# Where the old state of a chunked recurrence is added: in the PSUM accumulators or on VectorE

## The reference, cut to what matters

```python
def wkv_scan(r, w, k, v, a, bb, s0, reverse):
    def step(s, inp):
        r_t, w_t, k_t, v_t, a_t, b_t = inp
        sa = jnp.einsum("bhvk,bhk->bhv", s, a_t)
        s = s * w_t[:, :, None, :] + sa[..., None] * b_t[:, :, None, :] + v_t[..., None] * k_t[:, :, None, :]
        return s, jnp.einsum("bhvk,bhk->bhv", s, r_t)
    ...
    s_fin, o = lax.scan(step, s0, xs, reverse=reverse)
    return s_fin, jnp.moveaxis(o, 0, 1)
```

## Time and profile before

| what | us |
|---|---|
| median of 3 runs (lowest, highest) | 3789.93 (3787.76, 3793.22) |
| the profiled execution, own time | 3785.12 |
| its span | 3783.3 |
| TensorE busy in the span | 3357.8 (89%) |
| VectorE busy in the span | 2569.7 (68%) |
| ScalarE busy in the span | 1265.4 (33%) |

### The profile page before, as it was taken

The page is one execution under the profiler, slowest core; times in us unless marked ns, Lnnn a source line. Parts: engine busy times, 40 slices in busy tenths (PEclk is TensorE's granted clock), DMA queues, the critical chain, the costliest instruction groups (busy, mean ns, idle before and its releaser), DMA issues. The chain is left out here.

```text
span 3783.3 us, 67165 instructions
## 1 busy us (share of the span) xinstructions
PE 3357.8 (89%) x28642; PEld 2684.9 (71%) x28642; DVE 2569.7 (68%) x3589; ACT 1265.4 (33%) x2021; POOL 269.8 (7%) x235
## 2 busy tenths in 40 slices
PE   2999898999757877869999999989977999999997
PEld 1888686887426777737888888767735777888885
DVE  7566447572456676645977777767786588777777
ACT  2211222223434333323422222235465443222223
POOL 0000000000000000000111111020000001111110
PEclk9999999999869899979999999999968999999998
DMA  4233311132382233132111111111000121111111
GB/s 186 98 111 114 133 62 45 67 108 82 134 282 55 58 82 82 49 141 86 54 51 57 61 51 51 39 46 34 18 12 1 62 72 51 52 51 51 51 51 56
DMA packets 151062, 278.38 MB, mean 74 GB/s; under 512 B 9836, under 2 KB 82684, under 8 KB 150508
## 3 DMA queue, kind: packets, MB, share of 16 engines
q1 hardware_dynamic: 135468, 244.50, 19.5%
q10 hardware_dynamic: 15296, 29.57, 2.2%
HBM read 228.11 MB, written 45.65 MB: 72 GB/s over the span
## 5 line engine op out<-in xcount | busy, mean ns | idle before, releaser
L2518 PE MATMUL PS<-ffn_x_low_again,ring_b_wh 128*128 128x512 f32 x1120 | 436.0, 389 | 0.0
L2517 PE MATMUL PS<-ffn_x_high,ring_b_wh 128*128 128x512 f32 x1120 | 436.0, 389 | 0.0
L2767 DVE SCALAR_TENSOR_TENSOR xT<-xT,PS 128x1024 f32<-128x1024 f32 (+1 forms) x320 | 368.2, 1162 | 5.3 <-PE PS L2527 0.2
L248 DVE TENSOR_TENSOR ring_a_wl<-ring_a_raw,ring_a_wh 128x1024 fp32r<-128x1024 f32 x72 | 88.2, 1225 | 340.2 <-ACT ring_a_wh L245 339.9
L2750 DVE TENSOR_TENSOR xT<-xT,PS 128x512 f32<-128x512 f32 x280 | 188.1, 683 | 120.6 <-PE PS L2519 119.1
L245 ACT ACTIVATE ring_a_wh<-ring_a_raw 128x1024 fp32r<-128x1024 f32 x72 | 76.1, 1058 | 571.5 <-PE PS L282 547.2
L2525 PE MATMUL PS<-ffn_hid_high,ffn_down_high 128*128 128x512 f32 x640 | 253.2, 396 | 3.7 <-DVE xT L2767 3.2
L245 ACT ACTIVATE ring_b_wh<-ring_b_raw 128x512 fp32r<-128x512 f32 (+1 forms) x156 | 120.4, 773 | 388.7 <-PE PS L2519 252.9
L2526 PE MATMUL PS<-ffn_hid_low,ffn_down_high 128*128 128x512 f32 x640 | 250.3, 391 | 0.0
L2527 PE MATMUL PS<-ffn_hid_high,ffn_down_raw_again 128*128 128x512 f32 x640 | 250.2, 391 | 0.0
L2517 PEld LDWEIGHTS PS<-ffn_x_high,ring_b_wh 128*128 128x128 f32 x1120 | 210.3, 188 | 43.7
(11 more groups left out here) (507 smaller groups left out, 7767.3 us busy)
## 6 DMA issues: line engine op xcount, KB each, us to landing
ffn_down_raw<-in_ffn_down SPq DMA_DIRECT2D x40, 512.0 KB, 3.5
scan_tin<-scan_in SPq DMA_DIRECT2D x36, 512.0 KB, 5.3
norm_e_t<-in_ada SPq DMA_DIRECT2D x32, 512.0 KB, 4.0
ring_a_raw<-in_in_o SPq DMA_DIRECT2D x32, 512.0 KB, 4.4
ring_b_raw<-in_ffn_up SPq DMA_DIRECT2D x58, 256.0 KB, 4.5
ring_b_wl_again<-in_ffn_up SPq DMA_DIRECT2D x56, 256.0 KB, 4.3
scan_in<-um SPq DMA_DIRECT2D x20, 641.0 KB, 9.4
ring_a_raw<-in_in_e SPq DMA_DIRECT2D x24, 512.0 KB, 3.5
```

The costliest lines, as they stand in the source:

```text
L2517: nc.tensor.matmul(out, wh[:, k, :], xh[:, o, k], start=k == 0, stop=False)
L2518: nc.tensor.matmul(out, wh[:, k, :], xl[:, o, k], start=False, stop=False)
L2767: nc.vector.scalar_tensor_tensor(x, x, ALPHA if q == N_PLAIN else 1.0, out, ALU.mult, ALU.add)\
```

## The change

The old state enters PSUM by products: ahead of the growth's first `across`, the identity (128 x 128) times the state of each direction (128 x 256) goes into banks 2 and 3 with `start=True`, and both halves of the growth accumulate on it. VectorE's addition is gone; its scaling now reads the banks instead of `ST`.

```diff
@@ -1569,11 +1569,9 @@
                                     next(ahead, None)
                                 dve.wait_ge(S["u_done"], g * (4 * NC) + (4 * c + 4))
                                 st = ST[:, :, :, :]
-                                link(nc.vector.tensor_tensor(st.rearrange("p d j v -> p d (j v)"),
-                                                             st.rearrange("p d j v -> p d (j v)"), two_banks(2, 256),
-                                                             ALU.add))
                                 factor = fold[:, p, 1] if c == 0 else fold[:, 1 - p, 0]
-                                nc.vector.tensor_tensor(st, st, factor.unsqueeze(3).to_broadcast([P, 2, JB, HALF]),
+                                grown = two_banks(2, 256).rearrange("p d (j v) -> p d j v", j=JB)
+                                nc.vector.tensor_tensor(st, grown, factor.unsqueeze(3).to_broadcast([P, 2, JB, HALF]),
                                                         ALU.mult).then_inc(S["st_ready"], 1)
                             for _ in ahead:
                                 pass
@@ -1852,9 +1850,12 @@
                                 if not last_turn:
                                     turn_over(g + 1, 1 - p, 4 * c, 4 * c + 2)
                                 if not end:
+                                    for d in range(2):
+                                        nc.tensor.matmul(bank(2 + d, 256), ident[:, :], ST[:, d].rearrange("p j v -> p (j v)"),
+                                                         start=True, stop=False, skip_group_check=True)
                                     across(2, lambda j, h, d: tok[halves[d], p, T_K, c, j, halves[h]],
                                            lambda j, h, d: tok[halves[d], p, T_V, c, j, halves[h]], None, False,
-                                           stop=False, begin=True)
+                                           start=False, stop=False)
                                 pe.wait_ge(S["sa_ready"], g * NC + (c + 1))
                                 if not end:
                                     across(2, lambda j, h, d: tok[halves[d], p, T_B, c, j, halves[h]],
```

## The result

The changed kernel's median is 3803.71 us (6 runs) against 3792.35 for the kernel before (6 runs): ratio 1.0032, 95% interval 1.0021 to 1.0042, that is 8 to 16 us slower. In a second measurement it was 3795.57 (11 runs) against 3785.06 (24 runs), ratio 1.0027 (1.0017 to 1.0037), 6 to 14 us. The forecast was 3800 us (+10.3) with a range from 3792 to 3806.

What follows compares the result with a forecast made beforehand. In main turns' state parts TensorE was taken to work without pause, VectorE's update hidden. Updates summed to +11.3 us, stops took off 1.0: 3789.9 + 10.3 = 3800 us, range 3792 to 3806.

Steps and rivals of the forecast that it cites:

- The price of a pair: Two wide products ahead of the growth: four records 0.21 us apart, as at line 212, so 0.85 us.
- Hidden whole in main turns: VectorE's 1.42 us update in main turns delays nothing; slack before the state's products grows from 0.8 to about 1.5 us.
- Context turns: Updates of turns 0 and 1: first chunks +0.15 us each, second chunks, up to the masks, -0.2 each.
- Last turn: First chunk's update: the wait for SA partly covers the products, growth only some 0.4 us later; -0.3 us.
- The tie at the masks: Second chunks of turns 2 to 8: VectorE and TensorE arrive together at the next masks; some 0.2 us gained in all.
- TensorE's stops: Waits for the next instruction in the scan: four of the 14 main-turn places have one that pays, 1.05 us together.
- the rival's mechanism: Instruction pieces arrive on their own schedule, so later stops in the scan pay 6.7 us: +4.6, 3794.5 us; chance 0.18.
- the 11.3 - 1.0 of the sum: All updates: +11.7 main turns, +0.3 and -0.4 context turns, -0.3 last turn, less 1.0 from stops; net +10.3 us.
- that clock rival: In the scan, added TensorE work keeps the clock up and gives the loss back, 3789.6 us; chance 0.08.
- a growth of 1.7 us a turn: Sign of being right: from turn 2 to turn 9 the distance of like places grows so much, less stops.
- a scan longer by under 5 us: Sign of being wrong: if the scan grows by less than this, the sum was wrong in its main term.
- the main term: The 14 updates of main turns 2 to 8: TensorE pays 0.85 us each, less 0.2 in all, +11.7 us.

Runs made afterwards that it cites:

- no_add: Kernel before without the addition and without the wide products, so the old state is left out of the new one: 3781.36 us, ratio 0.9991.
- add_kept: Kernel before with the wide products put in front of the growth, which overwrites them, and VectorE's addition kept: 3796.89 us, ratio 1.0032.
- twice: Changed kernel with each pair of wide products issued twice: 3807.95 us, ratio to the kernel before 1.0059.
- the two context kernels: `context_ahead` and `context_only`, the kernel before with the change in the two context turns alone: 3789.10 and 3794.56 us.
- outputs_later: Kernel before with the second chunk's output products behind the next turn's first 16 products and remaining decays behind VectorE's third mask: 3784.53 us, ratio 0.9983.
- later_and_context: `outputs_later` plus the wide products in the two context turns, ahead of the wait for Z: 3782.08 us, ratio to the kernel before 0.9974.
- ahead_of_z: Changed kernel with the wide products one place earlier, ahead of the wait for Z: 3796.23 us, ratio to the kernel before 1.0020.
- context_ahead: Kernel before with the change in the two context turns alone, wide products ahead of the wait for Z: 3789.10 us, ratio 1.0001.
- context_only: Kernel before with the change in the two context turns alone, products at the change's place: 3794.56 us, ratio 1.0018.

## Why the prediction was right, point by point

*The price of a pair*: 0.85 forecast from line 212, 0.86 to 0.87 measured, and 0.87 for a second one. From the first wide record to line 1812 pass 0.95 us (1376.03 to 1376.98), not the 0.85 that the prediction named as a sign: the step from a wide product to the quarter products takes 0.31. But the wide products start 0.11 behind the last transpose, where the growth started 0.20 behind it, and 0.95 + 0.11 - 0.20 = 0.86.

*Hidden whole in main turns*: shown three ways. `no_add` leaves A at 3.93 where no stop stands, `add_kept` costs what the changed kernel costs, and the state is ready 1.05 us early. Forecast was a slack of 1.5; it is smaller because in this turn the stops went: from the copy of SA, the update starts 0.91 us later than before (3.09 against 2.18), but TensorE's next state product only 0.43 (4.83 against 4.40).

*Context turns*: A in turn 1 went from 3.74 to 3.89 (+0.15, as forecast; in the changed kernel's third profile it is 4.85, at a mean granted clock of 0.81 in that stretch). From SA to the masks it went from 3.00 + 2.32 to 3.86 + 1.25, -0.21 (forecast -0.2).

*Last turn*: A from 3.15 to 3.10, -0.05 (forecast -0.3): the update starts 2.26 us behind the copy of SA instead of 1.59, 0.67 later where 0.4 was forecast. Here, too, the pair stands between quarter products. Before, with the rest in the earlier trace rows:

```profile
1631.07 0.28 PE L1814 MATMUL PS<-tok 64*64 64x64 f32 x2
...
1631.43 0.69 DVE L1563 COPY SA<-PS 128x512 f32<-128x512 f32 x1 [1.59 <-PE PS L1739]
...
1631.97 0.38 PE L1814 MATMUL PS<-tok 64*64 64x64 f32 x9 [0.28 <-issue]
```

And in the changed kernel:

```profile
1638.26 1.13 PE L1854 MATMUL PS<-ST,ident 128*128 128x256 f32 x4
1638.37 0.69 DVE L1563 COPY SA<-PS 128x512 f32<-128x512 f32 x1 [2.02 <-PE PS L1737]
...
1639.32 0.69 PE L1812 MATMUL PS<-tok 64*64 64x64 f32 x32
...
1639.84 0.65 PE L1812 MATMUL PS<-SA,tok 64*64 64x64 f32 x32
```

The growth's first half starts 0.95 behind the start of the copy of SA instead of 0.36 ahead of it, 1.31 later and not 0.85. The half that reads SA starts 1.47 behind it instead of 0.75: the wait for SA, with a stop inside it, covered 0.6 us.

*The tie at the masks*: forecast -0.2 in seven turns. The distance from line 1731 to the masks adds up to 10.3, 10.9 and 10.2 us in turns 3 to 9 before, and 9.4 and 10.0 after: -0.8. Only a small part of that is the tie. In the first profile VectorE is late for the masks of turns 4 (1.39) and 6 (1.26), 0.15 us together, as forecast (the prediction counts by the turn before, 3 and 5). The rest are stops of TensorE inside the products that the masks wait for, in turn 7 before (2.64, 2.92 and 2.10 in the three profiles) and in turn 3 after (1.93 and 2.48), of which the prediction's list of turns says nothing. Turn 7 before, and turn 3 after:

```profile
1491.68 1.54 PE L1731 MATMUL PS<-AR,Bc 64*64 64x128 f32 x48 [1.20 <-issue]
...
1492.46 1.33 DVE L1509 COPY_PREDICATED LMB<-masks,PS 128x1024 f32<-128x1024 int32 x1 [1.74 <-PE PS L1731]
```

```profile
1283.83 1.31 PE L1729 MATMUL PS<-AR,Bc 64*64 64x128 f32 x36 [0.37 <-issue]
...
1284.30 1.34 DVE L1509 COPY_PREDICATED LMB<-masks,PS 128x1024 f32<-128x1024 int32 x1 [1.72 <-PE PS L1729]
```

In the other turns after, the context turns among them, the distance is 1.25.

*TensorE's stops*, the term that was mis-sized. Over turns 2 to 8, A adds up to 28.8, 29.4 and 28.9 us before and 34.1 and 34.4 after, +5.2; B to 29.8, 29.4 and 30.3 against 33.6 and 33.6, +3.8. Fourteen pairs at 0.86 would be 12.0, so 3.0 us were paid from stops inside the state parts, not 1.0. The prediction took the idle time that the profile notes for the price of a stop, and a stop lengthens its part by more. In turn 4 a stop of 0.16 is noted, but A is 4.40, 0.47 over the 3.93 of a part without one. The four places that the prediction counted with 1.05 us are 0.36, 0.47, 0.75 and 0.43 over 3.93, 2.0 together. Five more are 0.13 to 0.41 over it, 1.4 together, with no stop noted there or one under the 0.15 from which the views note idle time. All of them lie behind the product's place. In the changed kernel they are gone, and one new stop stands ahead of the place, in turn 8 (A 5.19 and 5.47). With 0.86 us more in each part the next piece seems to arrive in time; `twice`, with 1.73 more, has no stop in these parts either. That is the rival's mechanism at less than half of its size (6.7). Over the whole scan the noted stops fell by little, from 30.5 us in the mean to 29.2, so whether the 3.0 us were saved or part of them came back in the first parts of the turns is open.

Together the state parts and masks give +8.2 in main turns and some -0.1 in the others: +8.1, against the 11.3 - 1.0 of the sum. The scan as a whole is 5.7 longer, so 2.4 us came back in the rest of the turns, where the changed kernel's profiles have 10 us less of low clock on average (17 against 27). The forecast let that clock rival have 0.08; a small share of it was seen, but five profiles with 20 to 37 against 14 to 20 don't show that the products cause it, and the kernels without wide products in the main turns had 17 (`no_add`), 10 and 14 (the two context kernels), 24 and 10 us (`outputs_later`, `later_and_context`) of low clock, against 20, 17 and 14 in `add_kept`, `twice` and `ahead_of_z` with them. So low clock in the scan goes by neither. `context_ahead` had a clock of 0.99 over its main turns:

```profile
1270.00:1640.00 370.00, 287.60 (x11042) 264.18 (x11038) 233.66 (x381) 139.12 (x284) 10.53 (x24) 0.99 0.24 64
```

*Signs that did not come.* The prediction named a growth of 1.7 us a turn, less stops, from turn to turn. The state parts grew by 1.3 a turn, but from turn 3's first products to the last copy of SA it was 355.9 to 358.2 us before and 361.5 and 362.7 after, 0.7 a turn. And a scan longer by under 5 us was to mean that the main term is wrong; it is 5.7, not far above. The main term stands all the same, by the distances of the single places and by `twice`.

*What stays open, and what was luck.* The timed difference is 6 to 16 us over both measurements, the scan's 5.7. Outside the scan, profiles of the kernel before and of the changed one differ by 2.2 us in the mean (span less scan, 3276.8 against 3279.0), and those of the kernel before among themselves by up to 11.7. So 1 to 5 us of the timed difference have no place that the traces name. The trait is not this change's alone: in all nine edited kernels the timed difference to the kernel before is 1 to 10 us above that of the scan. The mechanism and the price of a pair were forecast rightly, but the forecast put all of its 10.3 us into the scan, where 5.7 were found, so that the total met the timed one (+10.5) to 0.2 us is luck.

## What to carry to other kernels

Before work is moved from one engine to another, look who waits at the place: an update for whose input VectorE waits 12 times in 19 and for whose output TensorE waits 3 times in 19 is nearly free where it stands, and costs its full price on the engine that doesn't pause. A cheap bound is the run that leaves the step out: it gave 3.7 us here (0 to 7), less than the 12 us that 14 pairs at 0.86 cost. The trace that shows an operation hidden also shows behind what (here output products ahead of the masks that everybody waits for), and moving that gave 6.4 us (2 to 10). And the idle time that a view notes at a stop is not its price: compare the distance between two fixed points with that of a place without a stop.

## What the runs showed of the hardware

- A float32 product over 128 x 128 weights with 256 moving columns takes 0.43 us in a row of such products: 4 records in 0.86, 8 in 1.73 (2.61 less 0.88). Behind transposes over the whole array a pair costs 0.86; between 64 x 64 products (`ahead_of_z`) 1.0 to 1.2.
- VectorE's 128 x 512 float32 multiplication lasts 0.69 us whether it reads the state from SBUF or from two PSUM banks.
- TensorE's stops for its next instruction are not a fixed toll: their places move with the program. In the stretches with 14 added pairs 3.0 of 12.0 us were paid from them, while the noted stops of the whole scan hardly fell (30.2, 29.0, 32.2 us before, 26.8 and 31.5 after). A noted stop of 0.16 us lengthened its part by 0.47.
- The scan of one kernel repeats within 1.0 us (512.5, 512.7, 511.7) or 1.3 us (517.3, 518.6) from profile to profile, though its time at the lower clock goes from 20 to 37 us. Kernels whose main turns are as in the kernel before differ by more from it (`context_only` 507.7, `context_ahead` 507.2), and only the second has a forecast gain; how the instructions lie may be part of that, which no run tested.
